# Expert weights of a mixture-of-experts encoder layer: one 2 MB transfer for each weight in place of two of 1 MB

## What is computed

```python
def expert_block(args):
    xblk, e = args                       # 128 tokens of one expert e, width 1024
    hid = jax.nn.silu(xblk @ w_gate[e]) * (xblk @ w_up[e])     # 1024 -> 512
    return hid @ w_down[e]                                     # 512 -> 1024
yb = lax.map(expert_block, (xb, block_e)).reshape(P, D)
y = jnp.zeros((T + 1, D), h.dtype).at[slot_tok].add(yb * slot_w[:, None])
```

## Time and profile before

| | us |
|---|---|
| median of 3 runs | 2146.08 |
| lowest and highest of them | 2141.89, 2154.14 |
| the profiled execution: its own time | 2152.06 |
| the profiled execution: span of the trace | 2150.2 |
| mean granted TensorE clock | 0.991 of full speed |

### The profile page before, as it was taken

One profiled execution on the slowest core, in us unless ns is written; L12 is line 12 of the kernel. 1 busy time (PEld: TensorE's weight loads), 2 busy tenths in 40 slices (PEclk: granted clock), 3 DMA queues, 4 the chain that ended last, 5 costly groups with the idle time before them and its releaser, 6 DMA issues.

```text
span 2150.2 us, 30216 instructions
## 1 busy us (share of the span) xinstructions
PE 2092.8 (97%) x10268; PEld 1730.2 (80%) x10268; DVE 1303.7 (61%) x1645; ACT 1073.8 (50%) x1582; POOL 511.6 (24%) x653
## 2 busy tenths in 40 slices
PE   8999999999999999999999999989999999999997
PEld 7788888888788888897888888757788788878886
DVE  5654233465555233555643434458899999899994
ACT  4453333343442332344523232137787788778884
POOL 4251011220541011213500012113212234332221
PEclk9999999999999999999999999999999999999999
DMA  7213222433213323452122225579999998997973
GB/s 229 92 40 98 88 87 92 173 130 108 74 40 108 98 79 98 163 171 69 40 85 82 81 96 205 206 271 357 386 395 394 394 340 299 392 384 262 325 260 88
DMA packets 108657, 396.72 MB, mean 184 GB/s; under 512 B 9282, under 2 KB 15603, under 8 KB 82964
## 3 DMA queue, kind: packets, MB, share of 16 engines
q1 hardware_dynamic: 91812, 335.64, 42.0%
q0 software_dynamic: 16752, 59.83, 10.5%
HBM read 402.78 MB, written 34.60 MB: 203 GB/s over the span
## 4 chain that ended last, share of the span: by engine, by line
PE 42%; DMA 10%; DVE 2%; issue 2%; ACT 2%; SPq 0%; POOL 0%; POOLq 0%; ACTq 0%; DVEq 0%
DMA held_wu<-w_up_e 5%; PE main L512 3%; PE main L514 3%; PE main L513 3%; DMA y<-e_yo,e_prv 2%; PE main L500 2%; PE main L502 2%; PE main L501 2%; PE main L1988 2%; PE main L1990 2%; PE main L1989 2%; DMA e_xg<-h2s,e_nxt 2%; PE main L1976 2%; PE main L1975 2%; PE main L1974 2%
## 5 line engine op out<-in xcount | busy, mean ns | idle before, releaser
L959 DVE TENSOR_TENSOR w_lo<-raw,w_hi 128x1024 fp32r<-128x1024 f32 (+1 forms) x216 | 250.3, 1180 | 320.3 <-ACT w_hi L705 320.2
L705 ACT ACTIVATE w_hi<-raw 128x1024 fp32r<-128x1024 f32 (+1 forms) x216 | 211.7, 1006 | 141.9 <-PE main L514 73.9
L512 PE MATMUL main<-e_g_hi,w_hi 128*128 128x512 f32 x576 | 237.6, 413 | 0.0
L514 PE MATMUL main<-e_g_hi,w_lo 128*128 128x512 f32 x576 | 226.1, 392 | 0.0
L513 PE MATMUL main<-e_g_lo,w_hi 128*128 128x512 f32 x576 | 225.4, 391 | 0.0
L500 PE MATMUL main<-w_hi,e_g_hi 128*128 128x512 f32 (+1 forms) x560 | 203.6, 364 | 2.3 <-DVE e_g_lo L973 2.3
L502 PE MATMUL main<-w_hi,e_g_lo 128*128 128x512 f32 (+1 forms) x560 | 200.2, 357 | 0.0
L501 PE MATMUL main<-w_lo,e_g_hi 128*128 128x512 f32 (+1 forms) x560 | 200.0, 357 | 0.0
L2097 DVE TENSOR_TENSOR e_d_lo<-held_wd,e_d_hi 128x2048 fp32r<-128x2048 f32 x76 | 173.1, 2288 | 36.2 <-ACT e_d_hi L2034 36.1
L2097 DVE TENSOR_TENSOR e_u_lo<-held_wu,e_u_hi 128x2048 fp32r<-128x2048 f32 x76 | 173.7, 2285 | 25.6 <-ACT e_u_hi L2034 25.6
L2097 DVE TENSOR_TENSOR e_g_lo<-held_wg,e_g_hi 128x2048 fp32r<-128x2048 f32 x76 | 173.5, 2283 | 2.5 <-ACT e_g_hi L2034 2.4
(11 more groups left out here) (349 smaller groups left out, 4786.5 us busy)
## 6 DMA issues: line engine op xcount, KB each, us to landing
held_wg<-w_gate_e SPq DMA_DIRECT2D x78, 1024.0 KB
held_wu<-w_up_e SPq DMA_DIRECT2D x78, 1024.0 KB
held_wd<-w_down_e SPq DMA_DIRECT2D x76, 1024.0 KB
raw<-w_in SPq DMA_DIRECT2D x120, 512.0 KB, 3.6
raw<-w_proj_b SPq DMA_DIRECT2D x24, 512.0 KB, 3.6
raw<-w_proj_a SPq DMA_DIRECT2D x24, 512.0 KB, 3.6
raw<-w_out SPq DMA_DIRECT2D x24, 512.0 KB, 4.2
raw<-w_in SPq DMA_DIRECT2D x24, 256.0 KB, 4.6
```

What stands on the lines that cost most here:

```text
L512: pe.matmul(bank[:], hi[:, k, :], mov_hi[:, k, :], start=(k == 0), stop=False)
L514: mm = pe.matmul(bank[:], lo[:, k, :], mov_hi[:, k, :], start=False, stop=(k == KT - 1))
L705: act.activation(hi, buf, ACT.Copy).then_inc(w_hi_done, 1)
L959: dve.tensor_tensor(lo, buf, hi.bitcast(F32), ALU.subtract).then_inc(w_split, 1)
```

## The change

`load_weights` moves the whole weight in one transfer, with one semaphore for each weight. SP waits for the low parts of both halves of the buffer's former contents, and reads the table once for a weight. ACT's `split_hi` of either half waits for the whole weight. The order of the weights in SP's program, the splitting in halves on ACT and DVE, and all other engines' programs stay as they were; the weights of the chosen blocks and of the mixers too.

```diff
-def load_weights(sp, a, held, w, h, e, new=None):
+def load_weights(sp, a, held, w, e, new=None):
     dst, name = held["w" + w], {"g": "w_gate_e", "u": "w_up_e", "d": "w_down_e"}[w]
-    k = dst.shape[1] // 2
-    src = a[name][bass.ds(e, 1), :, :].rearrange("o (p k) c -> p (o k) c", p=P)[:, h * k:(h + 1) * k, :]
-    sp.dma_start(dst[:, h * k:(h + 1) * k, :], src, cond=new, bounds_check=None).then_inc(held[f"w{w}_in"][h], 16)
+    src = a[name][bass.ds(e, 1), :, :].rearrange("o (p k) c -> p (o k) c", p=P)
+    sp.dma_start(dst, src, cond=new, bounds_check=None).then_inc(held[f"w{w}_in"], 16)
...
-        def load(i, w, h):
+        def load(i, w):
             e = sp.value_load(tab[0:1, bass.ds(i * TW + TW, 1)], min_val=0, max_val=NE - 1)
             new = sp.value_load(tab[0:1, bass.ds(i * TW + TW + 1, 1)], min_val=0, max_val=1)
-            sp.wait_ge(lo_done[w], i * 2 + (h + 1 if w == "d" else h - 1))
+            sp.wait_ge(lo_done[w], i * 2 + (2 if w == "d" else 0))
             sp.sem_inc(settled, 1)
-            load_weights(sp, a, held, w, h, e, new)
+            load_weights(sp, a, held, w, e, new)
...
-        load(1, "u", 0)
-        load(1, "u", 1)
-        load(2, "g", 0)
-        load(2, "g", 1)
-        load(1, "d", 0)
-        load(1, "d", 1)
-        load(2, "u", 0)
-        load(2, "u", 1)
+        load(1, "u")
+        load(2, "g")
+        load(1, "d")
+        load(2, "u")
         with sp.Fori(1, m + 1) as i:
-            for w, h in (("g", 0), ("g", 1), ("u", 0), ("u", 1)):
-                load(i + 2, w, h)
-            for h in range(2):
-                load(i + 1, "d", h)
+            load(i + 2, "g")
+            load(i + 2, "u")
+            load(i + 1, "d")
...
-            act.wait_ge(w_in[w][h], (i + 2) * 16)
+            act.wait_ge(w_in[w], (i + 2) * 16)
```

More of the change, by code:

```diff
@@ L289, in mixers @@
     held["main"], held["aux"], held["out_ready"], held["l_done"] = main, aux, out_ready, l_done
-    held["wg_in"], held["wu_in"], held["wd_in"] = x_first_in[0:2], x_first_in[2:4], [g_in_in, ident_in]
+    held["wg_in"], held["wu_in"], held["wd_in"] = x_first_in[0:3]
     hi_done, lo_done = held["hi_done"], held["lo_done"]
@@ L410, in sync @@
         load_chosen(sp, a, held, 1, "d")
-        for h in range(2):
-            load_weights(sp, a, held, "g", h, 0)
+        load_weights(sp, a, held, "g", 0)
     def tensor(pe):
@@ L1916, in sync @@
         m = blocks(sp)
-        def load(i, w, h):
+        def load(i, w):
             e = sp.value_load(tab[0:1, bass.ds(i * TW + TW, 1)], min_val=0, max_val=NE - 1)
             new = sp.value_load(tab[0:1, bass.ds(i * TW + TW + 1, 1)], min_val=0, max_val=1)
-            sp.wait_ge(lo_done[w], i * 2 + (h + 1 if w == "d" else h - 1))
+            sp.wait_ge(lo_done[w], i * 2 + (2 if w == "d" else 0))
             sp.sem_inc(settled, 1)
-            load_weights(sp, a, held, w, h, e, new)
-        load(1, "g", 0)
-        load(1, "g", 1)
+            load_weights(sp, a, held, w, e, new)
+        load(1, "g")
         sp.wait_ge(s_down_ps, 1)
-        for h in range(2):
-            load_weights(sp, a, held, "u", h, 0)
+        load_weights(sp, a, held, "u", 0)
         sp.wait_ge(s_down_ps, 2)
-        for h in range(2):
-            load_weights(sp, a, held, "d", h, 0)
-        load(1, "u", 0)
-        load(1, "u", 1)
-        load(2, "g", 0)
-        load(2, "g", 1)
-        load(1, "d", 0)
-        load(1, "d", 1)
-        load(2, "u", 0)
-        load(2, "u", 1)
+        load_weights(sp, a, held, "d", 0)
+        load(1, "u")
+        load(2, "g")
+        load(1, "d")
+        load(2, "u")
         with sp.Fori(1, m + 1) as i:
-            for w, h in (("g", 0), ("g", 1), ("u", 0), ("u", 1)):
-                load(i + 2, w, h)
-            for h in range(2):
-                load(i + 1, "d", h)
+            load(i + 2, "g")
+            load(i + 2, "u")
+            load(i + 1, "d")
         for w, ahead in (("g", 1), ("u", 1), ("d", 0)):
-            for h in range(2):
-                sp.wait_ge(w_in[w][h], m * 16 + (ahead + 3) * 16)
-                sp.sem_inc(settled, 1)
+            sp.wait_ge(w_in[w], m * 16 + (ahead + 3) * 16)
+            sp.sem_inc(settled, 1)
     def tensor(pe):
```

## The result

| | before | after |
|---|---|---|
| median, us | 2146.84 | 2203.66 |
| lowest and highest of 4 runs | 2141.89, 2154.14 | 2197.16, 2208.61 |
| profiled execution: span of the trace | 2150.2 | 2206.2 |

The changed kernel is slower: ratio 1.0247, 95% interval 1.0214 to 1.0281, +57 us where +16.5 was forecast. The direction and the start were as predicted, the size was not.

A forecast was written before the change was run, and what follows sets the result against it. Two close limits were seen: PE at 17.72 us a block and the weights' DMA queue at 18.57. Late landings gave 15.0 us, the second full stretch 1.5: +16.5 us, 2162.6 against the median; range 2148 to 2186.

The forecast's parts named there:

- d(1): Down's weight for block 1: asked for at 1465.4 us instead of 1460.06, leaving the queue idle 5.3 us more.
- u(3): Up's weight for block 3: asked for at 1489.1 us instead of 1475.69, leaving the queue dry for 6.0 us.
- the predicted gaps before 1500 us: Start of the stage: the weights' queue stands idle 5.3 us and then 6.0 us, with DMA share well under 1.
- Rate and number of transfers: DMA engines and SP's issues: no gain in rate; fewer issues gain 0, at most 2 us once.
- rival 3: Larger transfers save their fixed part, the DMA-paced stretch disappears and gathers come in time: about 2135 us; chance 0.06.
- Does the queue stay full?: DMA-paced stretch: up is asked for at 15.1 us, down keeps the queue busy until 18.6; 1.5 us margin remains.
- its order and bytes are the old ones: DMA-paced stretch: once never empty, the queue keeps its old order and bytes; everything lands 11.3 us late.
- Rival 2: The queue runs dry in each block, losing 1 us in some 20 blocks with new experts: 2182 us; chance 0.17.
- Its sign: A DMA share under 1 in the DMA-paced stretch would show that the queue runs dry in each block.
- The second stretch: Second full stretch, about 1825 to 1930 us: half 0's lateness costs 0 to 3.7 us, taken as 1.5.
- The clock term: Granted clock after a longer wait at 1476 us: may add 1.5 us to PE's path, which is covered.

## Why the prediction was wrong in size

**Right.** Up's half 0 was what PE waited on at the start: 10.6 and 8 us were predicted for the first two waits, 11.70 and 7.39 came. Asking moved as worked out: d(1) at 1465.4 predicted and at 1463.22 found, in a trace whose stage began 3.2 us earlier; u(3) at 1489.1 and 1485.95:

```profile
1463.22 0.33 SPq L1861 DMA_DIRECT2D held_wd<-w_down_e  x1
...
1485.95 0.33 SPq L1861 DMA_DIRECT2D held_wu<-w_up_e  x1
```

The two stretches that hold the predicted gaps before 1500 us have shares of 0.70 and 0.72. Rate and number of transfers gave no gain, so rival 3 fell; by the rule of the Trainium skill, SBUF — State Buffer, section "The DMA setup-cost knee", fewer and larger transfers would have been the better ones, and here two of 1 MB with the same waits are 14 us faster than one of 2 MB (2189.57 against 2203.36 and 2203.66).

**The step that failed** is the one under "Does the queue stay full?", with "The margin is 3.5 us, less the 2 us to the data: 1.5 us", and with it the term "its order and bytes are the old ones", a pace of 18.57 left as it was. Half of that step held. Landing to asking was reckoned at 15.1 - 6.2 = 8.9 us, and 8.95 was found. The rest of an 18.57 us block is 9.7 us for asking to landing; I reckoned 6.2 for the bytes and 2 to the data, 8.2. The trace has 8.2 as the least of 29 blocks, and 10.8 as the median. A margin of +1.5 us was in truth -1.1 at the median, and -1.9 in the block shown above (11.57). I took the best case of a transfer in an empty queue for one that shares 16 engines with the gather, the scatter and the weights asked for ahead of it. The lead of 3.5 us that the step gives up over gate's landing is right: 3.4 was found, with the gather moved ahead. What was wrong is that such a lead is enough for up to land 6.2 us after gate; it took 7.9, and these 1.7 us match the block's excess. (The text says that down keeps the queue busy until 18.6; by the order of the loads it is down and then gate.) A row of the prediction could have warned me: one gather had taken 15.4 us, and I priced it as bad luck. And for PE's own pace of 17.72 the limit is 8.8 us: so the eight blocks that were PE-paced before weren't safe either: in the changed kernel they took 17.7 to 21.7 us, 155.5 in all (1537.6 to 1693.0) in place of 141.7.

Rival 2 had the place right (each block with a new expert, by way of up's asking) and the price too low, 1 us a block: it was 20.27 - 18.57 = 1.7 us in the DMA-paced stretch, 2.5 against PE's pace. Its sign, a DMA share under 1 in the stretch, did not come, with 1.00; that the queue of weights runs dry there isn't shown.

**The second stretch** was given 1.5 us, since no wait for up stood there before. It lost 25. A buffer that isn't asked for until it is empty needs its whole round in every block; that PE had no wait there before said only that the halves had slack, not that the whole would. The longer waits bring a lower clock with them, as in the granted 0.74 and 0.86 of the first two stretches above; this is part of the waits' price, which I counted as covered.

**Clock and gathers.** The clock term (at most 1.5 us, "which is covered") can't be taken apart from the waits by these runs. The growth of the gather waits, from 8.5 to 31.7, goes with the 16 KB rows (with rows of 8 KB none were left), but without these waits the time is the same.

**Left open.** Why up, asked for 3.4 us before gate has landed, lands 7.9 us after it and not 6.2, with the DMA share at 1. How far up's round alone accounts for the loss, as 21 of 57 us come only with all three weights whole. Why one transfer of 2 MB is 14 us slower than two of 1 MB with the same waits. Asking to landing of up is 10.0 us (median of 22) with two and 10.5 with one at equal rows (32 blocks); that the difference is of this kind is seen, its mechanism is not.

## What to carry to other kernels

When a buffer has a single copy, write down its round: asking to landing under load, plus landing to the next asking; if that is more than the engine's time for a block, it sets the pace, however full the queue looks. Splitting a buffer's transfer pays by overlapping the emptying of one half with the filling of the other, so price a merge by what it adds to the round, and take asking to landing as the median of like transfers in the busy stretch, not as bytes over rate; it changes a little with the moment of asking, as the 10.8 and 11.6 us above show. And a wait that disappears may come back on the next semaphore: only the run with the wait taken away says what it was worth.

## What the runs showed of the hardware

- Rows matter to what runs beside them: a scatter landed in a median of 13.6 us beside weights in rows of 16 KB, and 11.4 beside the same single transfers in rows of 8 KB.
- A DMA share near 1 is not a rate: 393 GB/s at 1.02 with rows of 8 KB, 363 at 1.02 with rows of 4 KB, 363 at 1.00 with rows of 16 KB. So a full share doesn't say that a block's bytes can't move faster. What fills the share was not tried apart.
- In the stretches with PE's waits of 11.70 and 7.39 us the granted clock was 0.74 and 0.86. The matmuls right behind such a wait are slower too: the transposition of the hidden rows took 1.09 and 1.12 us there, and 0.66 behind a wait of 2.14. So a long wait costs more than its own length.
